# One inverse level in two halves, with the next tile's q transposes, scores and gram set between them, in a gated-DeltaNet recurrence on one Trainium2 core

## The chip, the cores and the metric

The kernel runs on one core of a Trainium2 chip. The metric is device time in microseconds (us) of one execution. TensorE does the products (PE is its matmuls, PEld its weight loads), VectorE is DVE, ScalarE is ACT, GpSimd is POOL, and SP issues most of the transfers. Each engine works through its own queue in order; they meet at semaphores.

## What is computed

The reference is one layer of a streaming encoder: layer norm and modulation, one input projection, a state-space mixer beside a gated DeltaNet mixer, an output projection, and a feed-forward block. The change lies in the DeltaNet mixer alone, in the work on a chunk of 64 tokens, four heads of width 128:

```
A = jnp.where(strict, jnp.einsum('bhnid,bhnjd->bhnij', k_beta, k) * dmask, 0.0)
T = lax.linalg.triangular_solve(eye + A, eye, left_side=True, lower=True)
u = T @ v_beta
w = T @ (k_beta * jnp.exp(decay)[..., None])
qk = jnp.einsum('bhnid,bhnjd->bhnij', q, k) * dmask
def step(S, inp):
    u_n, w_n, qk_n, qd_n, kd_n, gl_n = inp
    v_new = u_n - w_n @ S
    o_n = qd_n @ S + qk_n @ v_new
    S = S * gl_n[..., None, None] + jnp.einsum('bhck,bhcv->bhkv', kd_n, v_new)
    return S, o_n
```

## The kernel before

The kernel works through the recurrence in nine tiles of 128 tokens: eight of the prompt (t = 0 to 7) and one of the running stream (t = 8), each with four heads. A tile's triangular inverse is built in levels, l = 0 to 5 (`LV` levels; 0 to 4 for t = 8): each level doubles the block size of the inverse. Levels 0 to 4 work on 64x64 quadrants, UP (partitions 0 to 63) and DOWN (64 to 127); level 5 joins the two halves with one quadrant per product.

`level(t, l)` (from L1087) makes two products, each over the four heads. The first, P, at L1105 (L1102 at level 5) multiplies the off-diagonal block `Lc` by the inverse so far, `Xc`. ACT copies each head's result out of PSUM to `Pb` (`keep_P`, L1259). The second, X, at L1114 and L1116 (L1110 at level 5) waits for that head's `Pb` and multiplies again. DVE adds the result into `Xc` (`grow_X`, L1484; a copy at L1481 for level 5), and the next level's P waits for it head by head. So a head goes around PE, ACT, PE, DVE once a level, and the four heads stand behind each other in each of the two products.

All this is fp32. A 128x128 fp32 matmul is two instructions in the records, a transpose is one. The level's products use 64x64 pieces of the array, everything else uses 128 rows.

Between the levels of tile t, PE is given work that the next tile n = t+1 needs, and some of the tile before:

- `turn_kq(n)`: four transposes of k (L1055) and four of q (L1059), behind level 0. ACT squares them for the norms (`squares_k` L1217, `squares_q` L1224), which stand behind `keep_P` of levels 1 and 2 in ACT's order; POOL makes the scales (`scales`, L1354 to L1360) once both are there.
- `turn_o(t-1)`: four transposes of the output (L1169), behind level 2.
- `scores(n)`: four products of k and q (L1065), behind level 3.
- `gram(n)`: four products of k with k (L1072), behind level 4; `coupling(n)` on DVE (L1434) makes `Am` from them and the scales.
- `ada_columns(t-1)`: four small products with 128x128 weights (L1163), right behind the gram, for the modulation vectors; not in tile 0.

Level 5 comes then, `turn_A(n)` (L1078), which needs `Am`, `turn_v(n)` (L1084), `state(t)` (L1127 to L1140) and `ada_rows(t)` (L1147). Tile 8 has no next tile, and its levels carry only the transposes of the output and `ada_columns`. The order is written out by hand in `gdn_pe`; the orders of the other engines are in `gdn_act`, `gdn_dve` and `gdn_pool`.

Of the kernel before, what the change touches and what calls it, by code (L numbers as in the profile page):

```python
# [25 lines left out]
HEADS, HD = 4, 128  # L26
# [70 lines left out]
def stream_step(nc, I, O, DR):  # L97
    ctx = ExitStack()
    with ctx:

        on = {name: ctx.enter_context(nc.semaphore(name)) for name in SIGNALS}
# [135 lines left out]
        def since(name, value):  # L237

            return COUNTED_ON[name][1] + count(value)
# [649 lines left out]
        def glu_last(pe, c):  # L889

            proj_block(pe, 0, R_GLU + 8, (c,), lambda n: pe.wait_ge(on["glu_mix"], 9), y_hi, y_lo, 4, [YCH[c]])
# [153 lines left out]
        def gdn_pe(pe):  # L1045


            def turn_kq(n):
                pe.wait_ge(on["stg"][n % 2], 16 * (n // 2 + 1))
                if n < 2:  # L1050
                    pe.wait_ge(on["g_vp"], n)
                else:
                    pe.wait_ge(on["mod_row"], ADA0 + n - 1)
                for h in range(HEADS):
                    last = pe.transpose(h4(5)[:, h, :], stg[:, n % 2, k_ + h, :], ident[:])  # L1055
                last.then_inc(on["g_T"], 1)
                pe.wait_ge(on["g_QK"], n)
                for h in range(HEADS):
                    last = pe.transpose(h4(6)[:, h, :], stg[:, n % 2, q_ + h, :], ident[:])  # L1059
                last.then_inc(on["g_T"], 1)  # L1060

            def scores(n):
                pe.wait_ge(on["g_n"], n * 2 + 2)
                for h in range(HEADS):
                    last = pe.matmul(h4(6)[:, h, :], stg[:, n % 2, k_ + h, :], stg[:, n % 2, q_ + h, :], start=True, stop=True)  # L1065
                last.then_inc(on["g_QKp"], 1)

            def gram(n):
                pe.wait_ge(on["dec_k"], since("dec_k", 1))
                pe.wait_ge(on["g_AC"], since("g_AC", n))  # L1070
                for h in range(HEADS):
                    last = pe.matmul(h4(7)[:, h, :], stg[:, n % 2, k_ + h, :], stg[:, n % 2, k_ + h, :], start=True, stop=True)  # L1072
                last.then_inc(on["g_KK"], 1)

            def turn_A(n):
                pe.wait_ge(on["g_A"], n * HEADS + HEADS)
                for h in range(HEADS):
                    last = pe.transpose(h4(7)[:, h, :], Am[:, h, :], ident[:])  # L1078
                last.then_inc(on["g_AT"], 1)

            def turn_v(n):
                pe.wait_ge(on["g_kdec"], n + 1)
                for h in range(HEADS):
                    last = pe.transpose(h4(5)[:, h, :], stg[:, n % 2, v_ + h, :], ident[:])  # L1084
                last.then_inc(on["g_T"], 1)

            def level(t, l):  # L1087

                x = t % 2
                if l == LV - 1:  # L1090
                    pe.wait_ge(on["g_AC"], since("g_AC", t + 1))
                else:
                    pe.wait_ge(on["g_L"], t * 2 + (2 if l else 1))
                if l == 0:
                    pe.wait_ge(on["g_X0"], t * 2 + 2)
                    pe.wait_ge(on["g_R"], t * HEADS)
                    pe.wait_ge(on["g_S"], t * HEADS)
                for h in range(HEADS):
                    if l:
                        pe.wait_ge(on["g_X"], lv(t, l - 1, h) + 1)  # L1100
                    if l == LV - 1:
                        last = pe.matmul(ps[h][DOWN, 0:HB], Lc[x][UP, l, h, :], Xc[x][UP, h, 0, :], start=True, stop=True)  # L1102
                    else:
                        for q in (UP, DOWN):
                            last = pe.matmul(ps[h][q, 0:HB], Lc[x][q, l, h, :], Xc[x][q, h, 0, :], start=True, stop=True)  # L1105
                    last.then_inc(on["g_P"], 1)
                for h in range(HEADS):
                    pe.wait_ge(on["g_Pb"], lv(t, l, h) + 1)
                    if l == LV - 1:
                        last = pe.matmul(ps[h][UP, P + HB:2 * P], Pb[DOWN, h, 0:HB], Xc[x][DOWN, h, 1, :], start=True, stop=True)  # L1110
                    else:
                        if l < top(t):
                            for q in (UP, DOWN):
                                pe.matmul(ps[h][q, P:P + HB], Xc[x][q, h, 1, :], Pb[q, h, 0:HB], start=True, stop=True)  # L1114
                        for q in (UP, DOWN):
                            last = pe.matmul(ps[h][q, P + HB:2 * P], Pb[q, h, 0:HB], Xc[x][q, h, 1, :], start=True, stop=True)  # L1116
                    last.then_inc(on["g_XX"], 1)

            def state(t):
                x, st = t % 2, state_of(t)  # L1120
                if t == 0:
                    pe.wait_ge(on["g_init"], 5)
                if t == PTILES:
                    pe.wait_ge(on["s_state"], 32)
                for h in range(HEADS):
                    pe.wait_ge(on["g_X"], lv(t, top(t), h) + 1)
                    pe.matmul(hb(h, 0), stg[:, x, k_ + h, :], Sst[:, st, h, :], start=True, stop=True).then_inc(on["g_kS"], 1)  # L1127
                pe.wait_ge(on["g_Xf"], since("g_Xf", t + 1))
                for h in range(HEADS):
                    pe.wait_ge(on["g_R"], t * HEADS + h + 1)  # L1130
                    pe.matmul(hb(h, 3), Xf[x][:, h, :], Rb[:, h, :], start=True, stop=True).then_inc(on["g_V"], 1)
                pe.wait_ge(on["g_qd"], t + 1)
                pe.wait_ge(on["g_QK"], t + 1)
                pe.wait_ge(on["g_mix"], t)
                pe.wait_ge(on["mod_cols"], ADA0 + t)
                for h in range(HEADS):
                    pe.wait_ge(on["g_Vb"], t * HEADS + h + 1)
                    pe.matmul(h4(4)[:, h, :], qd[x][:, h, :], Sst[:, st, h, :], start=True, stop=False)  # L1138
                    pe.matmul(h4(4)[:, h, :], QK[x][:, h, :], Vb[:, h, :], start=False, stop=True)
                    pe.matmul(hb(h, 1), kdec[x][:, h, :], Vb[:, h, :], start=True, stop=True).then_inc(on["g_kv"], 1)  # L1140
# [15 lines left out]
            def ada_columns(t):  # L1156
                pe.wait_ge(on["mod_row"], ADA0 + t + 1)
                pe.wait_ge(on["g_mix"], t + 1)
                if t == 2:
                    pe.wait_ge(on["mod_cols"], ADA0 + 2)  # L1160
                    gate_rows(0, 4)
                for q in range(4):
                    last = pe.matmul(ps[4][:, 2 * q:2 * q + 2], modrow2[:, q * P:(q + 1) * P], sel[:], start=True, stop=True)  # L1163
                last.then_inc(on["mod_T"], 1)

            def turn_o(t):
                pe.wait_ge(on["g_ob"], t + 1)
                for h in range(HEADS):
                    last = pe.transpose(h4(4)[:, h, :], ob[:, h, :], ident[:])  # L1169
                last.then_inc(on["g_oT"], 1)  # L1170

            glu_last(pe, 0)
            pe.wait_ge(on["glu_sig"], 12)
            pe.wait_ge(on["gate_d"], 3)
            turn_kq(0)
            glu_last(pe, 1)
            glu_last(pe, 2)
            scores(0)
            gram(0)
            pe.wait_ge(on["gates"], 1)  # L1180
            pe.wait_ge(on["glu_mix"], 12)
            pe.wait_ge(on["g_init"], 3)
# [1 line left out]
            turn_v(0)  # L1184
            for t in range(TILES):
                n, more = t + 1, t + 1 < TILES
                level(t, 0)
                if more:
                    turn_kq(n)
                level(t, 1)  # L1190
                level(t, 2)
                if t:
                    turn_o(t - 1)
                level(t, 3)
                if more:
                    scores(n)
                level(t, 4)
                if more:
                    gram(n)
                if t:  # L1200
                    ada_columns(t - 1)
                if more:
                    level(t, 5)
                    turn_A(n)
                    turn_v(n)
                state(t)
                if t < PTILES:
                    ada_rows(t)
# [1278 lines left out]
        def _(pe):  # L2487
# [40 lines left out]
            gates_project(pe)  # L2528
            glu_pe(pe)
            out = gdn_pe(pe)  # L2530
            wo_pe(pe, out)
            ffn_pe(pe)
# [322 lines left out]
```

## Time and profile before

| | us |
|---|---|
| median of three runs | 1453.12 |
| lowest and highest | 1451.94, 1454.38 |
| span of the profiled execution | 1453.1 |
| recurrence in it (tile 0's first product to the state of tile 8) | 396.9 to 594.3 |
| one tile, t = 2 to t = 6 | 22.5 |

A row of the timeline is one group of like instructions that follow each other: start, time from the first's start to the last's end, engine, line, operation. Groups overlap, since matmuls are pipelined: what a group costs PE is the distance from its start to the start of the next one, not its own length. The profiled execution has the same time as the median, so sums made in its rows can be added to 1453.1.

### The profile page before, as it was taken

How to read it: one execution, taken by the hardware profiler on the slowest of the kernel's cores; microseconds unless marked ns; L12 is line 12 of the kernel's file. 1: busy time of each engine (PE TensorE's matmuls, PEld its weight loads, DVE VectorE, ACT ScalarE, POOL GpSimd, SP SyncE). 2: the span in 40 equal slices, each digit the busy share in tenths (PEclk: the TensorE clock that was granted, in tenths of full speed). 3: DMA queues.
4: the chain of work that ended last, by engine and by line, in shares of the span. 5: the costliest groups of instructions: out<-in, count | busy, mean ns of one | idle time of the engine just before them, and what ended most of it. 6: DMA issues, size and time to landing. Idle time of an engine off the chain costs nothing.

```text
span 1453.1 us, 28832 instructions
## 1 busy us (share of the span) xinstructions
PE 1402.9 (97%) x10784; PEld 1269.7 (87%) x10784; DVE 898.0 (62%) x1486; ACT 599.4 (41%) x1431; POOL 491.7 (34%) x598
## 2 busy tenths in 40 slices
PE   6999899989899999999999999999999999999996
PEld 4799899988888888888799999999999988888664
DVE  5618796764457667787695555555545544665846
ACT  6524344436465666334633333233323333334241
POOL 3888866861133343322233212221221200000102
PEclk8999999999999999999999999999999999999999
DMA  9431434335545453522322222221222158576562
GB/s 328 127 104 47 113 99 123 107 84 159 157 144 181 132 163 113 180 90 79 95 61 82 82 75 75 73 88 60 81 81 84 36 192 276 174 251 233 182 224 74
DMA packets 159974, 185.59 MB, mean 128 GB/s; under 512 B 12732, under 2 KB 122112, under 8 KB 159872
## 3 DMA queue, kind: packets, MB, share of 16 engines
q1 hardware_dynamic: 156992, 172.49, 38.2%
q10 hardware_dynamic: 2880, 11.72, 2.1%
q8 instruction: 66, 1.08, 0.3%
q14 instruction: 36, 0.29, 0.1%
HBM read 147.23 MB, written 35.78 MB: 126 GB/s over the span
## 4 chain that ended last, share of the span: by engine, by line
PE 65%; DVE 4%; ACT 3%; issue 3%; POOL 1%; DMA 0%; POOLq 0%; ACTq 0%; DVEq 0%
PE bank L2155 29%; PE bank L2066 16%; PE bank L278 3%; PE bank L1651 2%; PE bank L1105 2%; PE bank L1114 2%; PE bank L1611 2%; PE bank L2074 1%; PE bank L1116 1%; ACT hp L1701 1%; PE bank L1147 1%; PE bank L1138 1%; DVE stat L1733 1%; ACT vp L1252 1%; DVE xt L1768 1%
## 5 line engine op out<-in xcount | busy, mean ns | idle before, releaser
L2155 PE MATMUL bank<-Tlo,rh 128*128 128x272 f32 x640 | 184.7, 289 | 0.0
L2155 PE MATMUL bank<-Thi,rh 128*128 128x272 f32 x640 | 184.2, 288 | 0.0
L2155 PE MATMUL bank<-Thi,rl 128*128 128x272 f32 x640 | 184.0, 288 | 0.0
L278 PE MATMUL bank<-hT_hi,whi 128*128 128x384 f32 (+1 forms) x504 | 167.8, 333 | 3.2 <-DVE wlo L268 1.9
L278 PE MATMUL bank<-hT_lo,whi 128*128 128x384 f32 (+1 forms) x504 | 165.9, 329 | 0.0
L278 PE MATMUL bank<-hT_hi,wlo 128*128 128x384 f32 (+1 forms) x504 | 165.8, 329 | 0.0
L2155 PE MATMUL bank<-hT_lo,rh 128*128 128x272 f32 x480 | 138.5, 289 | 0.0
L2155 PE MATMUL bank<-hT_hi,rl 128*128 128x272 f32 x480 | 138.4, 288 | 0.0
L2155 PE MATMUL bank<-hT_hi,rh 128*128 128x272 f32 x480 | 137.9, 287 | 0.0
L2010 POOL TENSOR_TENSOR sums<-raw 128x512 f32<-128x512 f32 x20 | 25.7, 1287 | 321.7 <-DVE rl L1896 303.9
L2155 PEld LDWEIGHTS bank<-Thi,rl 128*128 128x128 f32 x640 | 120.6, 188 | 0.0
L2155 PEld LDWEIGHTS bank<-Thi,rh 128*128 128x128 f32 x640 | 120.5, 188 | 0.0
L2155 PEld LDWEIGHTS bank<-Tlo,rh 128*128 128x128 f32 x640 | 120.4, 188 | 0.0
L1896 DVE TENSOR_TENSOR rl<-sums,rh 128x512 fp32r<-128x512 f32 x80 | 55.4, 693 | 87.6 <-ACT rh L1892 87.6
L278 PEld LDWEIGHTS bank<-hT_hi,whi 128*128 128x128 f32 x504 | 95.9, 190 | 5.1 <-issue 2.9
L278 PEld LDWEIGHTS bank<-hT_lo,whi 128*128 128x128 f32 x504 | 95.9, 190 | 0.0
L278 PEld LDWEIGHTS bank<-hT_hi,wlo 128*128 128x128 f32 x504 | 95.9, 190 | 0.0
L2066 PE MATMUL bank<-wd_hi,hid_hi 128*128 128x512 f32 x236 | 93.2, 395 | 0.0
L2066 PE MATMUL bank<-wd_hi,hid_lo 128*128 128x512 f32 x236 | 91.9, 389 | 0.0
L2066 PE MATMUL bank<-wd_lo,hid_hi 128*128 128x512 f32 x236 | 91.9, 389 | 0.0
L1892 ACT ACTIVATE rh<-sums 128x512 fp32r<-128x512 f32 x80 | 50.0, 626 | 98.9 <-PE bank L2155 87.7
L2155 PEld LDWEIGHTS bank<-hT_hi,rh 128*128 128x128 f32 x480 | 90.7, 189 | 0.0
(434 smaller groups left out, 3591.5 us busy)
## 6 DMA issues: line engine op xcount, KB each, us to landing
wd_raw<-w_down SPq DMA_DIRECT2D x52, 512.0 KB, 3.5
wada<-w_ada SPq DMA_DIRECT2D x12, 2048.0 KB, 9.3
raw<-w_up SPq DMA_DIRECT2D x40, 512.0 KB, 5.1
hid<-sil SPq DMA_DIRECT2D x40, 272.0 KB, 2.1
wraw<-w_in SPq DMA_DIRECT2D x21, 512.0 KB, 4.3
rows<-convrow ACTq DMA_DIRECT2D x16, 577.5 KB, 3.6
hid_raw<-hid SPq DMA_DIRECT2D x44, 192.0 KB, 3.6
wrx<-w_down SPq DMA_DIRECT2D x14, 512.0 KB, 3.5
```

Of the source, the lines that this page charges most:

```text
L278: last = nc.tensor.matmul(ps[banks[c]][:, 0:cw], w[:, slot, k * P:(k + 1) * P], a[:, k, c0:c0 + cw], start=(k == 0 and n == 0), stop=(k == ...
L1105: last = pe.matmul(ps[h][q, 0:HB], Lc[x][q, l, h, :], Xc[x][q, h, 0, :], start=True, stop=True)
L1114: pe.matmul(ps[h][q, P:P + HB], Xc[x][q, h, 1, :], Pb[q, h, 0:HB], start=True, stop=True)
L1116: last = pe.matmul(ps[h][q, P + HB:2 * P], Pb[q, h, 0:HB], Xc[x][q, h, 1, :], start=True, stop=True)
L1138: pe.matmul(h4(4)[:, h, :], qd[x][:, h, :], Sst[:, st, h, :], start=True, stop=False)
L1611: last = pe.matmul(ps[up_bank(1, j, c)][:, 0:cw], w[:, j, k * P:(k + 1) * P], a[:, k, c0:c0 + cw], start=(k == 0 and n == 0), stop=(k == K ...
L1651: last = pe.matmul(ps[2 * s + h][0:n, :], a[:, s, k * P:k * P + n], w[:, k, cols], start=(k == 0 and m == 0), stop=(k == KD - 1 and m == 2))
L1892: act.activation(ring_hi[slot4(m, n)], operand(i, n, m), ACT.Copy).then_inc(on["st_hi"], 1)
L1896: dve.tensor_tensor(ring_lo[slot4(m, n)], operand(i, n, m), ring_hi[slot4(m, n)].bitcast(F32), ALU.subtract).then_inc(on["st_lo"], 1)
L2010: pool.tensor_tensor(sums[:, S1, :], A(1, 0), A(1, 1), ALU.add).then_inc(on["st_sum"], 1)
L2066: last = pe.matmul(ps[DBANKS[t % 4][h]][0:n, :], a[sl][:, cols], w[sl][:, h * 512:(h + 1) * 512], start=(k == 0 and m == 0), stop=(k == FB ...
L2155: last = pe.matmul(ps[banks[c]][:, 0:NC], w[:, ks], a, start=(n < 3 and k == 0 and p == 0), stop=(k == 3 and p == 2), skip_group_check=True)
```

## The change

`level` becomes `level_P` (the first product of the four heads, with the waits ahead of it) and `level_X` (the second). `turn_kq` becomes `turn_k` and `turn_q`, and `turn_q`, `scores` and `gram` take a list of heads: two heads are done between P and X of levels 1, 3 and 4, the other two behind X. The semaphore of each step is raised with the last head, as before. `ada_columns(t-1)` moves from ahead of level 5 to between its P and X. The order of the other engines is the same, and so is the number of products.

```
-                level(t, 0)
+                level_P(t, 0)
+                level_X(t, 0)
                 if more:
-                    turn_kq(n)
-                level(t, 1)
-                level(t, 2)
+                    turn_k(n)
+                level_P(t, 1)
+                if more:
+                    turn_q(n, LOW)
+                level_X(t, 1)
+                if more:
+                    turn_q(n, HIGH)
+                level_P(t, 2)
+                level_X(t, 2)
                 if t:
                     turn_o(t - 1)
-                level(t, 3)
+                level_P(t, 3)
                 if more:
-                    scores(n)
-                level(t, 4)
+                    scores(n, LOW)
+                level_X(t, 3)
                 if more:
-                    gram(n)
+                    scores(n, HIGH)
+                level_P(t, 4)
+                if more:
+                    gram(n, LOW)
+                level_X(t, 4)
+                if more:
+                    gram(n, HIGH)
+                    level_P(t, 5)
                 if t:
                     ada_columns(t - 1)
                 if more:
-                    level(t, 5)
+                    level_X(t, 5)
```

On PE, in a tile with a next one and one before it, level 3 with its P (L1105), X (L1114 and L1116) and the scores (L1065) stood so, up to the P of level 4:

```order
L1105 MATMUL bank<-Xc_136,Lc_138 64x64 x8
L1114 MATMUL bank<-Pb,Xc_136 64x64 x2
L1116 MATMUL bank<-Xc_136,Pb 64x64 x2
L1114 MATMUL bank<-Pb,Xc_136 64x64 x2
L1116 MATMUL bank<-Xc_136,Pb 64x64 x2
L1114 MATMUL bank<-Pb,Xc_136 64x64 x2
L1116 MATMUL bank<-Xc_136,Pb 64x64 x2
L1114 MATMUL bank<-Pb,Xc_136 64x64 x2
L1116 MATMUL bank<-Xc_136,Pb 64x64 x2
L1065 MATMUL bank<-stg 128x128 x4
L1105 MATMUL bank<-Xc_136,Lc_138 64x64 x8
```

And on PE, the same place after the change (P is now L1112, X is L1124 and L1126, the scores are L1070):

```order
L1112 MATMUL bank<-Xc_136,Lc_138 64x64 x8
L1070 MATMUL bank<-stg 128x128 x2
L1124 MATMUL bank<-Pb,Xc_136 64x64 x2
L1126 MATMUL bank<-Xc_136,Pb 64x64 x2
L1124 MATMUL bank<-Pb,Xc_136 64x64 x2
L1126 MATMUL bank<-Xc_136,Pb 64x64 x2
L1124 MATMUL bank<-Pb,Xc_136 64x64 x2
L1126 MATMUL bank<-Xc_136,Pb 64x64 x2
L1124 MATMUL bank<-Pb,Xc_136 64x64 x2
L1126 MATMUL bank<-Xc_136,Pb 64x64 x2
L1070 MATMUL bank<-stg 128x128 x2
L1112 MATMUL bank<-Xc_136,Lc_138 64x64 x8
```

Two of the four score products moved ahead of X; levels 1 and 4 look the same, with the q transposes and the gram. On PE at level 5 the row of the gram, `ada_columns`, P, X and the transposes of `Am` stood so:

```order
L1072 MATMUL bank<-stg 128x128 x4
L1163 MATMUL bank<-sel,modrow_123 128x2 x4
L1102 MATMUL bank<-Xc_136,Lc_138 64x64 x4
L1110 MATMUL bank<-Xc_136,Pb 64x64 x4
L1078 MATMUL bank<-ident,Am 128x128 x4
```

And on PE after it, with the gram at L1078, `ada_columns` at L1173, P at L1109, X at L1120 and the transposes of `Am` at L1085:

```order
L1078 MATMUL bank<-stg 128x128 x2
L1109 MATMUL bank<-Xc_136,Lc_138 64x64 x4
L1173 MATMUL bank<-sel,modrow_123 128x2 x4
L1120 MATMUL bank<-Xc_136,Pb 64x64 x4
L1085 MATMUL bank<-ident,Am 128x128 x4
```

Two gram products stand ahead of P, and the four of `ada_columns` have moved between P and X.

## Rows read from the trace of the kernel before

**Rows 1.** The page's span, and its row for PE (busy us, share).

```profile
span 1453.1 us, 28832 instructions
...
PE 1402.9 (97%) x10784; PEld 1269.7 (87%) x10784; DVE 898.0 (62%) x1486; ACT 599.4 (41%) x1431; POOL 491.7 (34%) x598
```

**Rows 2.** Windows, tiles 0 and 4: us, busy us of PE, PEld, DVE, ACT, POOL, granted clock, DMA share.

```profile
395.00:418.20 23.20, 21.01 (x328) 19.22 (x328) 14.42 (x48) 14.30 (x68) 5.95 (x11) 0.85 0.57 191
...
485.75:508.20 22.45, 22.25 (x360) 18.97 (x360) 14.95 (x48) 13.86 (x71) 7.94 (x14) 1.00 0.49 154
```

**Rows 3.** Timeline of tile 4, PE: start us, length us, engine, line, operation.

```profile
489.34 0.66 PE L1055 MATMUL bank<-ident,stg 128*128 128x128 f32 x4
...
490.36 0.68 PE L1105 MATMUL bank<-Xc,Lc 64*64 64x64 f32 x16
491.02 0.33 PE L1114 MATMUL bank<-Pb,Xc 64*64 64x64 f32 x4
...
492.00 0.89 PE L1105 MATMUL bank<-Xc,Lc 64*64 64x64 f32 x16
492.72 0.28 PE L1114 MATMUL bank<-Pb,Xc 64*64 64x64 f32 x4
...
493.75 0.66 PE L1169 MATMUL bank<-ident,ob 128*128 128x128 f32 x4
494.34 0.68 PE L1105 MATMUL bank<-Xc,Lc 64*64 64x64 f32 x16
494.99 0.33 PE L1114 MATMUL bank<-Pb,Xc 64*64 64x64 f32 x4
...
496.07 1.16 PE L1065 MATMUL bank<-stg 128*128 128x128 f32 x8
497.16 0.68 PE L1105 MATMUL bank<-Xc,Lc 64*64 64x64 f32 x16
497.81 0.33 PE L1114 MATMUL bank<-Pb,Xc 64*64 64x64 f32 x4
...
500.77 0.67 PE L1102 MATMUL bank<-Xc,Lc 64*64 64x64 f32 x8
501.40 0.67 PE L1110 MATMUL bank<-Xc,Pb 64*64 64x64 f32 x8
502.01 0.66 PE L1078 MATMUL bank<-ident,Am 128*128 128x128 f32 x4
```

**Rows 4.** Timeline of tile 4, ACT and DVE (in brackets: idle before, and who ended it).

```profile
494.71 0.57 ACT L1259 ACTIVATE Pb<-bank 128x64 f32<-128x64 f32 x4 [0.53 <-PE bank L1105]
...
491.51 0.99 DVE L1484 TENSOR_TENSOR Xc<-Xc,bank 128x128 f32<-128x128 f32 x4 [1.77 <-PE bank L1116]
...
500.19 1.13 DVE L1434 SCALAR_TENSOR_TENSOR Am<-bank,sc,E 128x128 f32<-128x128 f32 x4 [0.89 <-PE bank L1072]
```

**Rows 5.** Timeline of tile 4, weight loads around the scores, and of `ada_columns`.

```profile
495.80 0.20 PEld L1116 LDWEIGHTS bank<-Xc,Pb 64*64 64x64 f32 x4
496.07 0.97 PEld L1065 LDWEIGHTS bank<-stg 128*128 128x128 f32 x8
497.16 0.54 PEld L1105 LDWEIGHTS bank<-Xc,Lc 64*64 64x64 f32 x16
...
499.78 0.97 PEld L1163 LDWEIGHTS bank<-sel,modrow 128*128 128x128 f32 x8
500.77 0.54 PEld L1102 LDWEIGHTS bank<-Xc,Lc 64*64 64x64 f32 x8
```

**Rows 6.** Timeline of tile 4, PE in the state part: every third matmul of a run.

```profile
506.08 0.39 PE L1138 MATMUL bank<-Sst,qd 128*128 128x128 f32 x2
...
506.75 0.39 PE L1138 MATMUL bank<-Sst,qd 128*128 128x128 f32 x2
```

**Rows 7.** Timeline of tile 0, PE: P of level 4, X of level 5.

```profile
407.85 0.68 PE L1105 MATMUL bank<-Xc,Lc 64*64 64x64 f32 x16
...
411.31 0.68 PE L1110 MATMUL bank<-Xc,Pb 64*64 64x64 f32 x8
```

More of the change, by code:

```diff
@@ L1045, in gdn_pe, with turn_k @@
         def gdn_pe(pe):
-            def turn_kq(n):
+            def turn_k(n):
                 pe.wait_ge(on["stg"][n % 2], 16 * (n // 2 + 1))
@@ L1056, in turn_kq, with turn_q, scores, gram @@
                 last.then_inc(on["g_T"], 1)
+            LOW, HIGH, ALL = (0, 1), (2, 3), (0, 1, 2, 3)
+            def turn_q(n, heads):
                 pe.wait_ge(on["g_QK"], n)
-                for h in range(HEADS):
+                for h in heads:
                     last = pe.transpose(h4(6)[:, h, :], stg[:, n % 2, q_ + h, :], ident[:])
-                last.then_inc(on["g_T"], 1)
-            def scores(n):
+                if h == HEADS - 1:
+                    last.then_inc(on["g_T"], 1)
+            def scores(n, heads):
                 pe.wait_ge(on["g_n"], n * 2 + 2)
-                for h in range(HEADS):
+                for h in heads:
                     last = pe.matmul(h4(6)[:, h, :], stg[:, n % 2, k_ + h, :], stg[:, n % 2, q_ + h, :], start=True, stop=True)
-                last.then_inc(on["g_QKp"], 1)
-            def gram(n):
+                if h == HEADS - 1:
+                    last.then_inc(on["g_QKp"], 1)
+            def gram(n, heads):
                 pe.wait_ge(on["dec_k"], since("dec_k", 1))
                 pe.wait_ge(on["g_AC"], since("g_AC", n))
-                for h in range(HEADS):
+                for h in heads:
                     last = pe.matmul(h4(7)[:, h, :], stg[:, n % 2, k_ + h, :], stg[:, n % 2, k_ + h, :], start=True, stop=True)
-                last.then_inc(on["g_KK"], 1)
+                if h == HEADS - 1:
+                    last.then_inc(on["g_KK"], 1)
             def turn_A(n):
@@ L1085, in turn_v, with level_P @@
                 last.then_inc(on["g_T"], 1)
-            def level(t, l):
+            def level_P(t, l):
                 x = t % 2
@@ L1106, in level, with level_X @@
                     last.then_inc(on["g_P"], 1)
+            def level_X(t, l):
+                x = t % 2
                 for h in range(HEADS):
@@ L1174, in gdn_pe @@
             pe.wait_ge(on["gate_d"], 3)
-            turn_kq(0)
+            turn_k(0)
+            turn_q(0, ALL)
             glu_last(pe, 1)
             glu_last(pe, 2)
-            scores(0)
-            gram(0)
+            scores(0, ALL)
+            gram(0, ALL)
             pe.wait_ge(on["gates"], 1)
```

## The prediction

> **What bounds the kernel now.** I read the page first: PE is busy for 1402.9 of 1453.1 us [rows 1], so the time is PE's, and a change in one stage is worth what it does to PE's queue there. The table of windows says the same of one tile of the recurrence: in tile 4 PE is busy for 22.25 of 22.45 us, while DVE has 14.95 and ACT 13.86 [rows 2]. "Busy" hides two kinds of loss, though, since a matmul's end is modelled. They show only in the distances between starts, so the timeline of one tile is the view on which all that follows rests.
>
> The first loss is a wait inside a level. P of level 3 starts at 494.34, and X at 494.99: 0.65 us [rows 3]. Its sixteen weight loads are through 0.54 us after the first [rows 5]. X then stands for Pb: ACT starts on head 0 0.37 us after P (494.71) [rows 4], and X follows its copy. Some 0.1 us of PE is empty there. The same 0.65 stands in levels 1 and 4, and 0.63 in level 5 (500.77 to 501.40). Where no other work lies between two levels, there is a second wait: from X of level 1 to P of level 2 is 0.98 us (491.02 to 492.00), with no gap, but that P takes 0.72 us (492.00 to 492.72), since each head of it stands for DVE's sum, whose four take 0.99 us [rows 3, 4]. Against the usual 0.65 that is 0.07 more.
>
> The second loss is at each change between the 64x64 pieces and the 128-row products. The last group of X's weight loads ends at 496.00 (495.80 and 0.20), and the scores' first load starts at 496.07, together with their first matmul, so that it hides behind nothing [rows 3, 5]. On the way back: four score products take 1.09 us until the next P starts (496.07 to 497.16). A product alone, in an unbroken run, takes 0.223 us (0.67 for three) [rows 6], so four are 0.89, and 0.20 is the way back. For transposes: eight take 1.02 (489.34 to 490.36), four take 0.59 (493.75 to 494.34), so one is 0.11 and the way back 0.15 [rows 3].
>
> **The change part by part.** Nothing is removed. Work moves into the 0.1 us holes, and pays for it with more changes of shape. I sum each stretch with these blocks: four transposes 0.59, two 0.37; two products 0.45 and 0.20, so 0.64 (1.09 less two times 0.223); X up to the start of such a block 1.08 (494.99 to 496.07); and P up to the start of such a block. That last one is not in the trace, since P is always followed by X. I take the end of P's weight loads, 0.54, and the 0.07 that X shows ahead of the scores: 0.61 [rows 3, 5]. Its bounds are 0.49, half of X's 0.98 without any gap, as if the block followed with no loss, and 0.65, where it is no better than the wait it replaces.
>
> Stretch A, from the k transposes to X of level 2. Before: 489.34 to 492.72, 3.38 us [rows 3]. After: four transposes 0.59, P 0.61, two transposes 0.37, X 1.08, two transposes 0.37, P of level 2 at the usual 0.65: 3.67. The second half block delays level 2's P to 1.45 us behind X's start; DVE's four sums end 1.48 behind it (491.51 and 0.99 less 491.02) [rows 3, 4], and P's last head stands about 0.35 behind its first, so the 0.07 is won. Change: +0.29.
>
> Stretch B, P of level 3 to P of level 4. Before: 494.34 to 497.16, 2.82. After: P 0.61, two products 0.64, X 1.08, two products 0.64: 2.97. Change: +0.15.
>
> Stretch C, P of level 4 to X of level 5. Before: 497.16 to 501.40, 4.24. After: 0.61, 0.64, 1.08, 0.64, then P of level 5 up to a block, 0.61, then ada_columns from its first load to the next shape, 0.99 (499.78 to 500.77) [rows 5]: 4.57. Change: +0.33. In this stretch ada_columns hung on the gram without a change of shape, and now has a pair of its own. In tile 0 there is no ada_columns: before 3.46 (407.85 to 411.31) [rows 7], after 0.61, 0.64, 1.08, 0.64 and 0.63, 3.60: +0.14.
>
> Tile by tile: +0.77 in tiles 1 to 7, +0.58 in tile 0, nothing in tile 8. Together 7 times 0.77 and 0.58: +6.0 us. Tile 0 begins at the lower clock (0.85 granted over its window [rows 2]); what is moved there is as long at either place, so I add nothing.
>
> Now who else waits. The moved steps issue no transfers. ACT's order has squares_q behind keep_P of level 2, and both q halves are now issued ahead of that P, so the squares stay where they were relative to it. The scales on POOL and the scores' own wait for the squares move along with level 2. Am is the one with a date: DVE starts on it 500.19, and ends 501.32, with the transposes of Am at 502.01: 0.69 us to spare [rows 3, 4]. After the change there are 0.20 (way back), 0.61, 0.99 and 0.61 behind the last gram product, 2.4 us, against about 0.4 until DVE starts (the gram's last product ends about 499.8) and 1.13 for its work: it is in time. keep_P of the later levels gets more time, not less. The waits that are added to PE's queue (one or two for each second half) stand for things that are there by then; X's wait for each head shows no gap either. State, ada_rows and all that comes after the recurrence are the same rows, later by the sum.
>
> The Trainium skill has two rules that part here. "TensorEngine Tiling (Array Packing)", section Key Properties, says that changing the tiling mode, as opposed to the tile, drains TensorE; that is a price on each half block, and by it the sum above stands. "TensorE: Matmul & The Clock Gate", section "Step-by-step: what each phase is for", says that weight loads are pulled ahead of running matmuls where row groups don't conflict or the background buffer takes them; by it a half block would cost its products alone. The trace has the first load of the scores start with its matmul, so it bears out the first at these changes.
>
> **The rivals.** (1) The new changes of shape cost nothing: weights are loaded ahead there, as within a run. Then P up to a block is 0.49, and only the old blocks keep their way back. A: 0.59, 0.49, 0.22, 0.98, 0.22, 0.65, 3.15 (-0.23). B: 0.49, 0.45, 1.08, 0.64, 2.66 (-0.16). C: 0.49, 0.45, 1.08, 0.64, 0.49 and 0.89, 4.04 (-0.20); tile 0's C 3.29 (-0.17). Together 7 times -0.59 and -0.56: -4.7, 1448.4 us. For it: P to block isn't in the trace. Against it: every change that is there has its gap. This is also what the pull-ahead rule of the skill's clock-gate page would give. It decides if a half block behind P takes under about 0.3 us for transposes and 0.5 for products.
>
> (2) Only the step from P into a block is free (0.49), and the way back costs what it does now. A +0.17, B +0.03, C +0.09 (tile 0: +0.02): 7 times 0.29 and 0.22, +2.3, 1455.4 us, which no measurement can tell from no change.
>
> (3) Am comes late. If the gram's second half, or the scales that go through ACT and POOL, slip by more than the 0.9 us left in my sum (2.4 less 1.53), the transposes of Am wait on DVE. At 0.6 us a tile on top of the sum that is 7 times 0.6 more: 1463.3 us. Against it: only moves of a few tenths of a us stand upstream.
>
> **How the numbers follow.** The forecast (five more pairs of shape changes a tile, 1457 to 1462 us, likeliest 1459.1) has 0.66; rival 1 0.13; rival 2 0.15; rival 3 0.06. The range reaches from 1451.0 to 1462.0: it holds the forecast and rival 2, and leaves rival 1 and rival 3 out. A difference of 0.2% (2.9 us) is about what a measurement of this kernel can tell from no change. Faster by more than that: 0.13, rival 1. Within it: 0.18, rival 2 and the lower edge of the forecast. Slower: 0.69.
>
> **What the profile of the changed kernel would show.** A tile's period goes from 22.5 to 23.2 us, with PE still busy throughout. From P to a half block 0.61 us, and weight load and matmul of the block start together; from two transposes to X 0.37, from two products 0.64. X never waits for Pb in levels 1, 3, 4 and 5, and P of level 2 goes in 0.65. If half blocks take 0.22 and 0.45, rival 1 is right. If the transposes of Am name DVE as what ended their wait in tiles 1 to 7, rival 3 is. The prediction is wrong in its root if tiles get shorter though the gaps at the changes of shape are there: then X's waits were worth more than the 0.1 us that I read.

## The result and the profile after

The changed kernel is slower: its median is 1460.99 us (1459.15 to 1462.35, five runs) against 1452.33 us for the kernel before in the same comparison, a ratio of 1.0059 (95% interval 1.0046 to 1.0071). A second comparison on other runs, below, gave 1459.28 against 1453.36 us, 1.0036 (1.0022 to 1.0049). The forecast of 6.0 us over 1453.1 is a ratio of 1.0041, and lies between the two ratios. The profiled execution has this on its page, where [rows 1] has 1453.1 and 1402.9:

```profile
span 1459.2 us, 28840 instructions
...
PE 1408.5 (97%) x10784; PEld 1271.8 (87%) x10784; DVE 894.0 (61%) x1486; ACT 598.6 (41%) x1431; POOL 491.0 (34%) x598
```

PE has as many instructions as before and is busy for 5.6 us more, which is most of the 6.1. Since an engine does not get more work by doing it in another order, the "busy" time itself has holes in it, and the timeline shows them. Here is tile 4 of the kernel after on PE, from the k transposes to the transposes of Am, to be held against [rows 3] (P is L1112 and L1109 now, X L1124 and L1120, q L1063, scores L1070, gram L1078, `ada_columns` L1173):

```profile
491.97 0.66 PE L1055 MATMUL bank<-ident,stg 128*128 128x128 f32 x4
492.56 0.68 PE L1112 MATMUL bank<-Xc,Lc 64*64 64x64 f32 x16
493.17 0.44 PE L1063 MATMUL bank<-ident,stg 128*128 128x128 f32 x2
493.54 0.33 PE L1124 MATMUL bank<-Pb,Xc 64*64 64x64 f32 x4
...
494.62 0.44 PE L1063 MATMUL bank<-ident,stg 128*128 128x128 f32 x2
494.98 0.68 PE L1112 MATMUL bank<-Xc,Lc 64*64 64x64 f32 x16
495.64 0.33 PE L1124 MATMUL bank<-Pb,Xc 64*64 64x64 f32 x4
...
496.72 0.66 PE L1179 MATMUL bank<-ident,ob 128*128 128x128 f32 x4
497.31 0.68 PE L1112 MATMUL bank<-Xc,Lc 64*64 64x64 f32 x16
497.92 0.71 PE L1070 MATMUL bank<-stg 128*128 128x128 f32 x4
498.56 0.33 PE L1124 MATMUL bank<-Pb,Xc 64*64 64x64 f32 x4
...
499.64 0.71 PE L1070 MATMUL bank<-stg 128*128 128x128 f32 x4
500.28 0.68 PE L1112 MATMUL bank<-Xc,Lc 64*64 64x64 f32 x16
500.89 0.71 PE L1078 MATMUL bank<-stg 128*128 128x128 f32 x4
501.53 0.33 PE L1124 MATMUL bank<-Pb,Xc 64*64 64x64 f32 x4
...
503.25 0.68 PE L1109 MATMUL bank<-Xc,Lc 64*64 64x64 f32 x8
503.86 1.05 PE L1173 MATMUL bank<-sel,modrow 128*128 128x2 f32 x8
504.84 0.67 PE L1120 MATMUL bank<-Xc,Pb 64*64 64x64 f32 x8
505.45 0.66 PE L1085 MATMUL bank<-ident,Am 128*128 128x128 f32 x4
```

P to a half block takes 0.61 us at each place (492.56 to 493.17, 497.31 to 497.92, 500.28 to 500.89). Two transposes cost 0.37, two products 0.64, X up to the next block 1.08. The weight loads of a half block start with its first matmul, so nothing hides them:

```profile
497.92 0.52 PEld L1070 LDWEIGHTS bank<-stg 128*128 128x128 f32 x4
```

The tile's period is read from one start of `ada_rows` to the next, L1147 before and L1157 after. A tile without an irregular hole has 22.43 us before (418.23 to 440.66 in tile 1) and 23.24 after:

```profile
418.33 1.92 PE L1157 MATMUL bank<-wada,csil4b 128*32 128x512 f32 x16
...
441.57 1.92 PE L1157 MATMUL bank<-wada,csil4b 128*32 128x512 f32 x16
```

The 6.1 us of the two profiles, added up: 0.6 less ahead of the recurrence; 0.7 more in tile 0 (396.31 to 418.33 for 396.91 to 418.23); 6.2 more in tiles 1 to 7 (164.05 for 157.88); 0.2 less from there to the output projection; nothing after it (858.0 us from its first product to the end in both). Of the 6.2, seven times 0.80 are the change's own. The other 0.6 are irregular: a stretch at the lower clock that the last section tells of, 1.07 us, less some 0.5, since the single holes of the kernel before are larger than those of the kernel after.

### The profile page after: what moved, and what is told of

It is laid out like the page before. It is cut to its first block, busy times and chain, and to the rows that moved or that the text cites. A ratio compares the mean times of both kernels' runs of the same rounds, so it can differ in the third digit from the quotient of the medians.

```text
span 1459.2 us, 28840 instructions
## 1 busy us (share of the span) xinstructions
PE 1408.5 (97%) x10784; PEld 1271.8 (87%) x10784; DVE 894.0 (61%) x1486; ACT 598.6 (41%) x1431; POOL 491.0 (34%) x598
## 3 DMA queue, kind: packets, MB, share of 16 engines
q8 instruction: 66, 1.08, 0.3%
## 4 chain that ended last, share of the span: by engine, by line
PE 65%; DVE 4%; ACT 3%; issue 3%; POOL 1%; DMA 0%; POOLq 0%; ACTq 0%; DVEq 0%
PE bank L2180 29%; PE bank L2091 16%; PE bank L278 3%; PE bank L1676 2%; PE bank L1112 2%; PE bank L1124 2%; PE bank L1636 2%; PE bank L2099 1%; PE bank L1126 1%; ACT hp L1726 1%; PE bank L1157 1%; PE bank L1078 1%; PE bank L1070 1%; PE bank L1148 1%; DVE stat L1758 1%
```

## The experiments

Two theories stood against each other. Theory 1, that of the prediction: every pair of changes between 64x64 pieces and 128-row products (into the other shape and back) has a price of some 0.3 us, wherever it stands. The change adds five pairs a tile, two with q and one each with the scores, the gram and `ada_columns`. For one half block it is 0.12 on the way in (0.61 for 0.49) and 0.20 on the way back (0.15 behind transposes), and the wait of P that the half block fills gives back up to 0.16 (0.65 for 0.49). Theory 2: it is X that must not come late behind its P, and the half blocks made it late. Each run is read by its period in tile 1, from which holes that come only in some tiles stay away, and by its ratio. Each period is from one profile; in every profile one of tiles 4 to 7 has the same within 0.01 us.

### The parts one by one

Each kernel is the one before with one part of the change. The order of steps in each tile, written short and only where it differs from the kernel before:

```
 q_only:      level_P(t, 1); turn_q(n, LOW); level_X(t, 1); turn_q(n, HIGH); level_P(t, 2)
 scores_only: level_P(t, 3); scores(n, LOW); level_X(t, 3); scores(n, HIGH); level_P(t, 4)
 gram_only:   level_P(t, 4); gram(n, LOW); level_X(t, 4); gram(n, HIGH); ada_columns(t - 1); level_P(t, 5)
 ada_only:    gram(n, ALL); level_P(t, 5); ada_columns(t - 1); level_X(t, 5)
```

> The kernel before with one part of the change: two q transposes stand between P and X of level 1 and two behind X; scores, gram and ada_columns stand as before. Theory 1 (each change between 64x64 pieces and 128-row products has its price, wherever it stands): the k transposes to X of level 2 take 3.67 us instead of 3.38 in a tile, the tile's period goes from 22.50 to 22.79, eight tiles +2.3 us. Theory 2 (a cost for what X is late behind its P, and none for the changes of shape; the 0.74 us a tile of the whole change shared out by how much later X starts, 0.33 us here of 2.46 in all): +0.10 us a tile, +0.8 us.

> The kernel before with one part of the change: two score products between P and X of level 3, two behind X. Theory 1: P of level 3 to P of level 4 takes 2.97 us instead of 2.82, eight tiles +1.2 us. Theory 2 (X is 0.60 us later of 2.46): +0.18 us a tile, +1.4 us. This run alone does not tell them apart; it is there for the sum of the parts.

> The kernel before with one part of the change: two gram products between P and X of level 4, two behind X, with ada_columns right behind them as before. Theory 1: P of level 4 to X of level 5 takes 4.40 us instead of 4.24 (0.14 more in tile 0), eight tiles +1.3 us. Theory 2: +0.18 us a tile, +1.4 us. There for the sum of the parts.

> The kernel before with one part of the change: ada_columns stands between P and X of level 5, the whole gram behind level 4 as before. Theory 1: the gram gets a way back of 0.20 us, P to ada_columns is 0.61, ada_columns to X 0.98: 4.42 instead of 4.24 us from P of level 4 to X of level 5, seven tiles +1.2 us. Theory 2 (X is 0.94 us later of 2.46): +0.28 us a tile, +2.0 us. The four parts together should give the whole change, +6.1 us by the profiles, if they don't act on each other.

Measured, with the starts of `ada_rows` of tiles 0 and 1 behind the period:

| kernel | period of tile 1 | more than before | median | ratio (95%) |
|---|---|---|---|---|
| before | 22.43 (418.23, 440.66) | | 1454.62 | |
| q_only | 22.77 (418.58, 441.35) | 0.34 | 1456.07 | 1.0009 (1.0000 to 1.0019) |
| scores_only | 22.58 (417.25, 439.83) | 0.15 | 1455.35 | 1.0011 (1.0001 to 1.0021) |
| gram_only | 22.58 (418.29, 440.87) | 0.15 | 1455.85 | 1.0004 (0.9994 to 1.0013) |
| ada_only | 22.60 (418.71, 441.31) | 0.17 | 1454.26 | 1.0002 (0.9992 to 1.0011) |

The parts add up: 0.81 us a tile, where the whole change has 0.81 in tile 1. Their sizes go with theory 1 (0.29, 0.15, 0.16, 0.18) and not with theory 2 (0.10, 0.18, 0.18, 0.28): q, whose X is the least late, costs the most, and it is the one that adds two pairs: a pair costs 0.15 to 0.17 in all four. With the scores that is the 0.32 of way in and way back less the 0.16 of the wait that the half block fills. By the clock of whole runs the parts are too small to be told from each other, and gram_only and ada_only can't be told from nothing; only the periods carry this.

### A pair of changes without a late X, and a late X without a pair

```
 scores_in_X:  level_P(t, 3); level_X(t, 3, LOW); scores(n, LOW); level_X(t, 3, HIGH); scores(n, HIGH)
 scores_whole: level_P(t, 3); scores(n, ALL); level_X(t, 3); level_P(t, 4)
```

> The kernel before, with the scores cut in two halves, but none of them between P and X: X of level 3 is made for heads 0 and 1, then two score products, then X for heads 2 and 3, then the other two. X is not later behind its P than before, and one pair of changes of shape is added. Theory 1 (the price stands on the changes): P of level 3 to P of level 4 takes 0.65, 0.61, 0.64, 0.61 and 0.64, 3.15 us instead of 2.82, eight tiles +2.6 us. Theory 2 (the price stands on X being late behind P): 2.82 or less, no slower than before.

> The kernel before, with all four score products between P and X of level 3 and none behind X: as many changes of shape as before, X later by 1.05 us. Theory 1: 0.61, 1.09, X without a gap 0.98, and P of level 4, which now stands for DVE's sums, 0.72 up to its X: 3.40 us from P of level 3 to X of level 4, where it was 3.47; eight tiles -0.6 us. Theory 2: X is late by nearly twice as much as with half a block (1.05 for 0.60), so +0.3 us a tile, +2.4 us.

The timeline of scores_in_X, level 3 of tile 4 on PE, where X begins 0.66 us behind P as before and is cut in two by the scores:

```profile
494.63 0.68 PE L1112 MATMUL bank<-Xc,Lc 64*64 64x64 f32 x16
495.29 0.33 PE L1124 MATMUL bank<-Pb,Xc 64*64 64x64 f32 x4
...
495.90 0.71 PE L1070 MATMUL bank<-stg 128*128 128x128 f32 x4
496.55 0.33 PE L1124 MATMUL bank<-Pb,Xc 64*64 64x64 f32 x4
...
497.16 0.71 PE L1070 MATMUL bank<-stg 128*128 128x128 f32 x4
497.80 0.68 PE L1112 MATMUL bank<-Xc,Lc 64*64 64x64 f32 x16
```

From P to P it is 3.17 us for 2.82 (expected 3.15), the period of tile 1 is 22.78, 0.35 more than before, the median 1456.23 against 1453.10 us, ratio 1.0018 (1.0008 to 1.0028). Half of X costs 0.61, that is 0.12 more than half of an unbroken 0.98; the two score products cost 0.64 or 0.65. X was not late behind P, and the price is there in full. Theory 2 has no room for this.

The timeline of scores_whole, tile 1 on PE, where X is 1.05 us later than before and no pair was added:

```profile
423.89 0.68 PE L1112 MATMUL bank<-Xc,Lc 64*64 64x64 f32 x16
424.50 1.16 PE L1070 MATMUL bank<-stg 128*128 128x128 f32 x8
...
426.57 0.89 PE L1112 MATMUL bank<-Xc,Lc 64*64 64x64 f32 x16
```

P to P is 2.68 (423.89 to 426.57), the period 22.30 (415.31 to 437.61), 0.13 less than before, where theory 1 expected 0.07 less and theory 2 0.30 more. P of level 3 to X of level 4 is 3.41 us (423.89 to 427.30; expected 3.40). The median is 1452.55 against 1453.10 us, ratio 0.9996 (0.9985 to 1.0006), which by itself can't be told from none. So filling the wait from P to X is worth about 0.1 us here by the period of a tile; what made it dear was the cut in halves, which adds a pair of changes of shape.

### One pair less, and work for a wait in the same shape

```
 scores_with_gram: level(t, 3); level(t, 4); gram(n); scores(n); ada_columns(t - 1)
 scores_in_state:  level(t, 3); level(t, 4); gram(n); ada_columns(t - 1)
```

In scores_in_state the scores stand in `state(t)`, between the product that makes V and the waits ahead of the loop over the outputs:

```diff
                     pe.matmul(hb(h, 3), Xf[x][:, h, :], Rb[:, h, :], start=True, stop=True).then_inc(on["g_V"], 1)
+                if t + 1 < TILES:
+                    scores(t + 1, ALL)
                 pe.wait_ge(on["g_qd"], t + 1)
```

> The kernel before, with the four score products behind the gram at level 4 and nothing behind level 3: one pair of changes less a tile. Theory 1: from P of level 3 up to ada_columns 5.21 us for 5.44, -0.23 us a tile, eight tiles -1.8 us. Theory 2 (changes of shape are free): nothing gained, and level 4's P stands for DVE, +0.07 us a tile, +0.6 us.

> The kernel before, with the four score products in the state part, between the product that makes V and the loop over the outputs, where PE waits for ACT's copy of V and all is 128 rows already; nothing stands behind level 3. Theory 1: P of level 3 to X of level 4 goes from 3.47 to 2.35 us (0.65, 0.98, 0.72), and V's product to the loop from 1.37 to 1.78 us, the four products being 0.89 and the hole some 0.5: -0.71 us a tile, eight tiles -5.7 us. Theory 2 (changes of shape are free, so that only the hole is won): -0.4 us a tile, -3.3 us. If the waits on ACT and DVE just move along, nothing is won.

Both missed. scores_with_gram has a period of 22.65 (416.58 to 439.23), 0.22 more than before instead of 0.23 less, median 1456.50 against 1453.10 us, ratio 1.0018 (1.0007 to 1.0029). scores_in_state has 22.20 (417.98 to 440.18), 0.23 less instead of 0.71 less, median 1452.46, ratio 0.9993 (0.9982 to 1.0003). In scores_with_gram the second theory had +0.07 us a tile, also less than was measured. The place is level 4; the timeline of scores_with_gram, tile 4, PE and then ACT:

```profile
495.48 0.89 PE L1112 MATMUL bank<-Xc,Lc 64*64 64x64 f32 x16
496.64 0.33 PE L1124 MATMUL bank<-Pb,Xc 64*64 64x64 f32 x4 [0.27 <-ACT Pb L1281]
...
494.69 1.27 ACT L1254 ACTIVATE E<-drow,gcol 128x128 f32<-128x128 f32 x4
495.86 0.62 ACT L1257 ACTIVATE erow<-drow 128x512 f32<-128x512 f32 x1
496.38 0.55 ACT L1281 ACTIVATE Pb<-bank 128x64 f32<-128x64 f32 x4
```

X comes 1.16 us behind P, not 0.72. With nothing between levels 3 and 4, ACT has to copy P of level 4 at about 495.9, but in its order the next tile's decay comes first: four operations for E and one for the row, 1.8 us in all, which the scores had covered on PE. That is 0.44 of the missing 0.45 in the one, and of the missing 0.48 in the other. The estimate had looked at PE alone and forgotten what its block was covering on ACT. So both kernels were made again with the row's operation, `erow` (0.62 us), taken out of `decay` and put behind the copies of level 4, as `decay_row`:

```diff
                     decay(n)
                     keep_P(t, 4)
+                    decay_row(n)
                     decay_exp(n)
```

In state_two_and_two, besides, two of the score products stand ahead of the product that makes V and two behind it. The whole change was run again beside them.

> The whole change once more, on the chip and beside the runs of the kernel before that the next three share. By its parts (0.34, 0.15, 0.15 and 0.17 us a tile in their own profiles, 0.81 together, and 23.23 less 22.43, 0.80, in its own) it should cost 6.2 us, a ratio of 1.0043. If a further cost of 2 to 3 us goes with it that no part has, the ratio stays at 1.0059 (medians 8.7 us apart), and it has to be found in rows outside the six levels. If that was scatter, the ratio comes down to 1.004 to 1.005.

> Scores in the state part as before, and one step of ACT put later: the exponential of a whole row (erow, 0.62 us), which stood ahead of the copies of level 4's P, now stands behind them. In the run without that, X of level 4 waited for ACT until 1.16 us behind its P, or 0.80 behind it where X of level 3 had been held up first. Theory 1 (a price on each change of shape, and ACT's row the only reason why the gain stayed out): P to X of level 4 comes down to 0.72 to 0.85 us, the tile's period from 22.20 to 21.8 or so, against 22.43 before: eight tiles -5 us, ratio 0.9965. Theory 2 (changes of shape free, only the hole of 0.5 won): period 22.1, -3 us. If it stays at 22.20, the wait at level 4 is not ACT's row.

> Scores behind the gram, one pair of changes of shape less, with ACT's row behind the copies of level 4's P, as in the run above. Without that its period was 22.65, 0.22 more than before. Theory 1: one pair less is worth 0.23 us, a delay of 0.1 may be left at level 4: period 22.20 to 22.32, -1 to -1.8 us. Theory 2: one pair less is worth nothing, 22.43 to 22.55.

> As the scores in the state part with ACT's row later, but two score products stand ahead of V's product, where PE waits for DVE's right sides some 0.1 us, and two behind it, where it waits for ACT's copy of V some 0.5 us. Theory 1: both holes are filled with work of the same shape, so the period is 0.1 us less than with all four behind V, 21.7, -0.8 us more over eight tiles. If V's copy is late for it, the period is the same or longer.

| kernel | period of tile 1 | against before | median | ratio (95%) |
|---|---|---|---|---|
| before | 22.43 | | 1453.36 | |
| change_again | 23.24 (417.32, 440.56) | +0.81 | 1459.28 | 1.0036 (1.0022 to 1.0049) |
| state_row_later | 21.72 (414.76, 436.48) | -0.71 | 1449.09 | 0.9967 (0.9954 to 0.9979) |
| gram_row_later | 22.16 (417.56, 439.72) | -0.27 | 1452.22 | 0.9991 (0.9982 to 1.0000) |
| state_two_and_two | 21.47 (414.60, 436.07) | -0.96 | 1446.90 | 0.9955 (0.9942 to 0.9968) |

With the row out of the way, P to X of level 4 is 0.72 us in both. A pair of changes less is worth what theory 1 said, and a little more (-0.27 for the -0.23 of the first estimate), and the scores in the state part too (-0.71 for -0.71, where theory 2 had -0.33). state_row_later and state_two_and_two are faster than the kernel before, by 0.33% and 0.45%; the interval of gram_row_later reaches 1.0000. No run has ACT's row moved alone; in the kernel before, X of level 4 doesn't wait for it (it stands 0.65 behind P, as in the other levels). The timeline of tile 1 of state_two_and_two on PE shows the gain: nothing between X of level 3 and P of level 4, and in the state part, all 128-row products, not one of the starts leaves a hole:

```profile
423.19 0.68 PE L1112 MATMUL bank<-Xc,Lc 64*64 64x64 f32 x16
...
424.82 0.89 PE L1112 MATMUL bank<-Xc,Lc 64*64 64x64 f32 x16
425.55 0.28 PE L1124 MATMUL bank<-Pb,Xc 64*64 64x64 f32 x4
...
430.62 1.06 PE L1137 MATMUL bank<-Sst,stg 128*128 128x128 f32 x8
431.51 0.61 PE L1070 MATMUL bank<-stg 128*128 128x128 f32 x4
431.96 1.06 PE L1143 MATMUL bank<-Rb,Xf 128*128 128x128 f32 x8
432.85 0.61 PE L1070 MATMUL bank<-stg 128*128 128x128 f32 x4
433.30 0.39 PE L1152 MATMUL bank<-Sst,qd 128*128 128x128 f32 x2
```

Two score products take 0.45 us here (431.51 to 431.96, 432.85 to 433.30), their bare price. Their first weights are loaded 0.11 us ahead of their first matmul, which the half blocks between P and X never have (497.92 above, load and matmul):

```profile
431.40 0.53 PEld L1070 LDWEIGHTS bank<-stg 128*128 128x128 f32 x4
```

The step has the same semaphore wait in PE's queue at either place, so the price between P and X is not one of that wait: between P and X of the changed kernel the same two take 0.64 and also cost P its step into another shape. Before, V's product went 1.37 us up to the loop, with the hole in it:

```profile
503.96 1.17 PE L1131 MATMUL bank<-Rb,Xf 128*128 128x128 f32 x8
505.33 0.46 PE L1138 MATMUL bank<-Sst,qd 128*128 128x128 f32 x2 [0.20 <-ACT Vb L1279]
```

The two ahead of V gained 0.25 us a tile where 0.1 was expected. With all four products behind V, two stretches before them had a loss: the product before V's (L1137) took 1.02 us up to V's (430.78 to 431.81 in state_row_later), and V's own took 1.00 (431.81 to 432.81), since each head of it stood for DVE's right side. With two products ahead of V both take the bare 0.89 (430.62 to 431.51, 431.96 to 432.85): 0.13 and 0.11, of which the expectation had counted one.

## Why the prediction was right

**What bounds it.** That PE's distances between starts set the time held throughout: no other engine's work got longer (DVE 894.0 us for 898.0, ACT 598.6 for 599.4, POOL 491.0 for 491.7), and the part behind the recurrence moved along unchanged.

**The blocks.** P up to a block, the one number that no row had, was taken as 0.61 with 0.49 and 0.65 as its bounds; it is 0.61. Stretch A is 3.67 (491.97 to 495.64; forecast 3.67), B 2.97 (497.31 to 500.28; 2.97), C 4.56 (500.28 to 504.84; 4.57). The +0.77 a tile came out as +0.80. The 0.03 between them is an end that the sum left out: once P of level 2 no longer stands for DVE, X behind it has to wait again and its first weights are not hidden (load and matmul both start at 495.64; before, the load stood at 492.66 and the matmul at 492.72), so from X to the output transposes it takes 1.08 us (495.64 to 496.72) where it had 1.03 (492.72 to 493.75 in [rows 3]). Of the 0.07 that stretch A was to win there, 0.05 goes back. q_only shows the same, 0.34 for 0.29. The same end is what scores_whole (-0.13 for -0.07) and gram_row_later (-0.27 for -0.23) won beyond their sums: there X of level 4 takes 1.03 us instead of 1.08 to the gram, behind a P that stands for DVE. The term is small, but it is one of the mechanism: the sum had a wait on DVE as a pure loss.

Tile 0 has +0.70 for +0.58, and there the sum had a block wrong. In tile 0 no output transposes stand ahead of level 3, so its P stands for DVE, and up to the half block it takes 0.82 us (404.62 to 405.44) and not 0.61. Stretch B is 3.18 (404.62 to 407.80) where it had 2.87 (404.98 to 407.85): +0.31 for +0.15. X of level 2 has 0.05 more, as in the other tiles; stretch A, where the clock rises, has +0.18 for +0.29 (399.07 to 403.64 for 399.66 to 404.05), C +0.14 as forecast.

**The waits.** The date of Am held. DVE starts on it 503.46 and takes 1.13 us, and the transposes start at 505.45, 0.86 us later than it ends:

```profile
503.46 1.13 DVE L1459 SCALAR_TENSOR_TENSOR Am<-bank,sc,E 128x128 f32<-128x128 f32 x4 [0.44 <-PE bank L1078]
```

So rival 3 did not come. Rival 1 (the changes of shape free) is refuted by every half block, and by scores_in_X; rival 2 (only the step behind P free) by the 0.61. Of the two rules of the Trainium skill that the prediction set against each other, the one of "TensorEngine Tiling (Array Packing)", Key Properties, that a change of tiling mode drains the engine, agrees with the trace: two products cost 0.45 us in one shape and 0.64 between two. The pull-ahead of weight loads of "TensorE: Matmul & The Clock Gate", section "Step-by-step: what each phase is for", is there within a shape and not across two: before, the first weights of level 2's P are loaded at 491.94, ahead of its first matmul at 492.00 [rows 3] and while X still runs, where those of a half block start with its matmul (497.92 above).

```profile
491.94 0.81 PEld L1105 LDWEIGHTS bank<-Xc,Lc 64*64 64x64 f32 x16
```

How much of the price is a drain, and how much the load that is not hidden, no run here tells apart.

**The size in whole runs.** The forecast was 6.0 us over the profile's 1453.1. By profile it is 6.1, by the second comparison's medians 5.9 (1459.28 less 1453.36; its ratio of 1.0036 makes 5.2), by the first one's 8.7. That the profile agrees to 0.1 us is luck in part: the change's own is 6.3 by the periods (seven times 0.80 and 0.70), the start of the recurrence and its end took 0.8 off that, and the irregular holes put 0.6 on. The 1459.1 us is built on a profile's span, and in every timed execution on record the span is 1.7 to 1.8 us less than the time. So the execution with the span of 1453.1 us was not one at the median: 1459.1 is to be held against the span after, 1459.2, and against the medians only the difference of 6.0. The two intervals overlap from 1.0046 to 1.0049. The kernel before alone had medians from 1452.33 to 1454.62 in the four comparisons, so what the first had on top is of the size of the scatter; more can't be said. The repeat was expected at 1.0043 if nothing but the parts is in it; its interval holds that, and excludes the 1.0059 of the first. Its period in tile 1 is the first profile's, 23.24.

**What the estimate of the experiments missed** lay on ACT: for the kernels with levels 3 and 4 side by side I had followed DVE's sums and not ACT's order, and lost 0.44 us a tile to it. The prediction had checked ACT for the change itself (copies get more time, not less), but had not asked which of ACT's work the blocks on PE were covering.

## What to carry to other kernels

Before putting work into a hole on TensorE, compare the hole with the price of getting there and back: here a wait of at most 0.16 us behind a 64x64 product was filled at 0.3 us for each additional pair of changes between array shapes. Between products of another shape, move a block whole, not in halves, and look first for waits in the stretches that already have its shape: the four score products alone, cut in halves around X, cost 0.15 us a tile; whole between P and X they won 0.13; in the state part, with one operation of ACT put later, they won 0.71, and 0.96 when cut in halves there, where a cut adds no change of shape. And when a block leaves a place, look at every engine for the work that it was hiding.

## What was not expected of the hardware

**A fall of the clock.** Both profiles of the whole change have one stretch in tiles 1 to 7 at the lower clock, and none of the other twelve profiles has (read from 420 to 585 us in stretches of 5 us, none under 0.98). In the first it is the end of tile 7 (windows view: us, busy us of PE, PEld, DVE, ACT and POOL, granted clock, DMA share, GB/s), and PE's transposes of Am, which take 0.49 us elsewhere until the next row, take 0.87:

```profile
575.00:578.70 3.70, 3.70 (x21) 3.63 (x20) 1.50 (x7) 2.27 (x7) 0.00 (x0) 0.54 0.00 0
...
575.14 1.07 PE L1085 MATMUL bank<-ident,Am 128*128 128x128 f32 x4
576.01 1.06 PE L1091 MATMUL bank<-ident,stg 128*128 128x128 f32 x4
```

In change_again it is the end of tile 6:

```profile
550.00:554.00 4.00, 4.00 (x27) 3.92 (x27) 1.28 (x7) 2.46 (x9) 0.00 (x0) 0.63 0.00 0
```

Each time it is the lower of the two levels, 1.2 of 2.4 GHz, and sets in right behind X of level 5, after a level 5 whose P and X were parted by `ada_columns`, whose products are two columns wide; it costs 1.07 and 1.01 us (tiles of 24.30 and 24.24 us for 23.23). PE was busy without a break in the 5 us before (5.00 of 5.00 us from 570 to 575, and from 546 to 551 in change_again).

Falls to the lower clock stand elsewhere too, in tile 8 and outside the recurrence. Three of them come behind waits of PE: gram_only has one in tile 8 from 592.1 us, scores_with_gram one from 591.0, each within 0.1 us of the start of V's product, ahead of which PE had been idle for 0.66 us, and the kernel before has one behind the recurrence from 702.2, after 1.85 us idle. The one of gram_only:

```profile
592.10:595.50 3.40, 3.40 (x16) 3.40 (x17) 1.85 (x6) 2.22 (x6) 0.00 (x0) 0.50 0.02 5
...
592.05 2.00 PE L1141 MATMUL bank<-Rb,Xf 128*128 128x128 f32 x8 [0.66 <-DVE Rb L1515]
```

ada_only has the same level 5 as the whole change and no fall in tiles 1 to 8, so the cause of the two falls is open: the rhythm of the whole tile, or chance; two profiles don't tell.

**Holes with no name.** Most profiles have single holes of 0.2 to 1.4 us in PE's weight loads that no wait explains, in tiles 3, 5 and 6 mostly: 0.57 us in the scores of tile 5 before, 0.22 in tile 3 after, and 1.07, 1.36 and 0.55 in gram_row_later, 3.0 us in all, more than its gain of eight times 0.27 us:

```profile
472.08 0.20 PEld L1112 LDWEIGHTS bank<-Xc,Lc 64*64 64x64 f32 x4 [1.07 <-issue]
```

Here P of level 3 stops after three heads for 1.07 us, with "issue" as the reason. What sets their place was not tried. They are one reason why a gain of 0.1% shown by the period of one tile need not show in the whole: of eight times 0.96 us, 7.7, the medians of state_two_and_two show 6.5.
